# A 248-column product whose result nobody reads, placed ahead of groups of four transposes

## What is computed

```
x = x + squared_relu_mlp(rmsnorm(x, mlp_norm_g[i]), mlp_w_up[i], mlp_w_down[i])   # first model
m = jax.nn.silu(c) @ ada_w + ada_b        # second model: 6 x 1024 modulation columns per layer
```

## Time and profile before

| | |
|---|---|
| median of 3 runs | 1195.76 us (1193.81 to 1197.41) |
| profiled execution, its own time | 1202.31 us |
| its span, first to last instruction | 1200.7 us |
| TensorE busy (matmul rows) | 1185.0 us, 99% of the span |
| VectorE busy | 863.5 us, 72% |
| ScalarE busy | 636.0 us, 53% |
| granted TensorE clock, mean | 0.999 |

### The profile page before, as it was taken

The page is one execution under the profiler, slowest core; times in us unless marked ns, Lnnn a source line. Parts: engine busy times, 40 slices in busy tenths (PEclk is TensorE's granted clock), DMA queues, the critical chain, the costliest instruction groups (busy, mean ns, idle before and its releaser), DMA issues.

```text
span 1200.7 us, 23381 instructions
## 1 busy us (share of the span) xinstructions
PE 1185.0 (99%) x9643; PEld 1148.8 (96%) x9643; DVE 863.5 (72%) x1143; ACT 636.0 (53%) x853; POOL 95.4 (8%) x147
## 2 busy tenths in 40 slices
PE   8999999999999999999999999999999999999998
PEld 8999999999998999999999999999988779999998
DVE  5776887778776897777899888886476557755443
ACT  7557566634447567634468464333455665543432
POOL 0000010110124011110200001110000000000000
PEclk9999999999999999999999999999999999999999
DMA  9442587887772588787844648876745406565361
GB/s 335 159 175 72 178 290 269 297 291 253 263 263 72 176 270 291 277 289 275 294 171 141 203 149 281 286 254 204 235 142 193 157 1 187 166 210 178 124 193 66
DMA packets 150009, 249.98 MB, mean 208 GB/s; under 512 B 5505, under 2 KB 80618, under 8 KB 149930
## 3 DMA queue, kind: packets, MB, share of 16 engines
q1 hardware_dynamic: 135810, 198.21, 49.1%
q0 software_dynamic: 13952, 50.60, 11.7%
q10 hardware_dynamic: 168, 0.04, 0.0%
HBM read 247.79 MB, written 1.05 MB: 207 GB/s over the span
## 4 chain that ended last, share of the span: by engine, by line
PE 88%; DVE 8%; ACT 2%; issue 1%; ACTq 0%; POOL 0%; DVEq 0%
PE ps L2137 26%; PE ps L2139 26%; PE ps L2138 26%; DVE w_lo L1252 4%; PE ps L2405 2%; PE ps L2275 1%; PE ps L2693 1%; DVE scratch L1729 1%; PE ps L2387 1%; PE ps L2191 1%; ACT h_both L804 1%; PE ps L2667 1%; PE ps L2374 1%; PE ps L2707 1%; PE ps L2218 0%
## 5 line engine op out<-in xcount | busy, mean ns | idle before, releaser
L1252 DVE TENSOR_TENSOR w_lo<-raw,w_hi 128x2048 fp32r<-128x2048 f32 (+4 forms) x196 | 412.6, 2144 | 103.0 <-ACT w_hi L737 102.8
L737 ACT ACTIVATE w_hi<-raw 128x2048 fp32r<-128x2048 f32 (+4 forms) x196 | 342.0, 1790 | 169.0 <-PE ps L2139 168.9
L2137 PE MATMUL ps<-h_both,w_hi 128*128 128x256 f32 (+1 forms) x1296 | 363.8, 281 | 2.9 <-issue 1.1
L2139 PE MATMUL ps<-h_both,w_lo 128*128 128x256 f32 (+1 forms) x1296 | 361.3, 279 | 0.0
L2138 PE MATMUL ps<-h_both,w_hi 128*128 128x256 f32 (+1 forms) x1296 | 361.3, 279 | 0.0
L2137 PEld LDWEIGHTS ps<-h_both,w_hi 128*128 128x128 f32 (+1 forms) x1296 | 242.7, 187 | 4.3 <-issue 3.8
L2138 PEld LDWEIGHTS ps<-h_both,w_hi 128*128 128x128 f32 (+1 forms) x1296 | 244.2, 188 | 0.1
L2139 PEld LDWEIGHTS ps<-h_both,w_lo 128*128 128x128 f32 (+1 forms) x1296 | 244.1, 188 | 0.0
L2137 PE MATMUL ps<-a_both,w_hi 128*128 128x256 f32 x864 | 242.1, 280 | 0.0
L2139 PE MATMUL ps<-a_both,w_lo 128*128 128x256 f32 x864 | 241.4, 279 | 0.0
L2138 PE MATMUL ps<-a_both,w_hi 128*128 128x256 f32 x864 | 241.3, 279 | 0.0
(11 more groups left out here) (420 smaller groups left out, 1823.6 us busy)
## 6 DMA issues: line engine op xcount, KB each, us to landing
ada_raw<-in_l_ada_w POOLq DMA_DIRECT2D x96, 512.0 KB, 6.7
raw<-in_mlp_w_up SPq DMA_DIRECT2D x32, 1024.0 KB, 6.9
raw<-in_mlp_w_down SPq DMA_DIRECT2D x32, 1024.0 KB, 6.8
raw<-in_l_ffn_w_gate SPq DMA_DIRECT2D x22, 1024.0 KB, 5.4
raw<-in_l_ffn_w_up SPq DMA_DIRECT2D x22, 1024.0 KB, 8.0
raw<-in_l_ffn_w_down SPq DMA_DIRECT2D x16, 768.0 KB, 6.0
raw<-in_l_w_qkv SPq DMA_DIRECT2D x12, 1024.0 KB, 7.0
raw<-in_l_w_in SPq DMA_DIRECT2D x10, 1024.0 KB, 6.5
```

The lines of the kernel that those rows point to most:

```text
L737: nc.scalar.activation(w_hi[:, s.slot, cut], raw[:, s.slot, cut], ACT.Copy).then_inc(split_hi, 1)
L1252: nc.vector.tensor_tensor(w_lo[:, s.slot, cut], raw[:, s.slot, cut], w_hi[:, s.slot, cut].bitcast(F32), ALU.subtract).then_inc(split_lo, 1)
L2137: nc.tensor.matmul(to, sh, mh, start=first, stop=False, skip_group_check=True)
L2139: return nc.tensor.matmul(to, sl, mh, start=False, stop=last, skip_group_check=True)
```

## The change

`ada_reduce` takes an optional pair of operands. If it is given, one more matrix instruction is issued behind the semaphore wait and before the four transposes: a float32r product of 248 columns into bank 7, where the first transposes then overwrite it. Nothing reads it. It is given in the loops of `two_bank_slot` with `reduce` and in the down product: 6 groups in the two up products, 8 in the two down products, 4 in the gate/up product of the third layer, 18 of 24 in all. Its stationary operand is the first block of the slot's `w_hi`, its moving one a chunk of the rounded activations that the products around it use. The six other groups (one before slot 1 and one behind the down product in each MLP, group 9, group 23) stay as they are.

```diff
-            def ada_reduce(group):
+            def ada_reduce(group, unread=None):
 
                 pe.wait_ge(ada_step, group * 8 + 8)
+                if unread is not None:
+
+                    w, x = unread
+                    nc.tensor.matmul(ps[:, ADA_BANK, 0:T - 8], w, x[:, 0:T - 8], start=True, stop=True, skip_group_check=True)
                 for q in range(4):
                     ins = nc.tensor.transpose(ps[:, ADA_BANK, q * P:(q + 1) * P],
                                               scratch[:, 2 + q // 2, (q % 2) * P:(q % 2 + 1) * P], ident[:, :])
...
                     if b and reduce is not None:
-                        ada_reduce(reduce)
+                        ada_reduce(reduce, (ring(w_hi, s.slot, s.kc, s.cols)[:, 0, 0:P], hi[:, 0, :]))
...
                             if b == 1 and j % 2 == 0:
-                                ada_reduce(ADA_GROUP[f"down{l}"] + 2 * i + j // 2 - 1)
+                                ada_reduce(ADA_GROUP[f"down{l}"] + 2 * i + j // 2 - 1,
+                                           (ring(w_hi, s.slot, s.kc, s.cols)[:, 0, 0:P], a_hi[:, KD * j, :]))
```

## The result

The changed kernel takes 1205.79 us (median of 8 runs, 1201.98 to 1210.4) against 1197.7 us for the one before (8 runs); the ratio is 1.0069 with a 95% interval of 1.0049 to 1.0090. The forecast was 1190.3 with a range up to 1202, so the sign was wrong and the time outside the range. The rival "all stretches slow" had said 1204.2.

What follows compares the result with a forecast made beforehand. TensorE, running back to back, was taken to bound the kernel. Added products +2.04 us, slow stretches turned fast -7.6 and products behind a down product turned slow +0.2 gave -5.4: 1190.3 us from the 1195.76 median, range 1187.5 to 1202.

Steps and rivals of the forecast that it cites:

- all stretches slow: Rival: product plus transposes leave the slow rhythm behind every changed group; +8.4 us, 1204.2 us; chance 0.15.
- it costs 0.11 us: Each of 18 added products, between back-to-back TensorE work, costs 0.113 us like a 256-column product; +2.04 us in all.
- The two rhythms: Between groups, TensorE's products follow each other every 113.5 or 117.7 ns; 0.80 us per stretch of 192 products.
- an unchanged group entered fast leaves slow: Behind the first layer's down product, the unchanged group makes 54 products up to the norm sum slow; +0.2 us.
- the term of -7.6 us: Slow stretches become fast if all 18 groups keep the fast rhythm: 6.0 us in both MLPs, 1.6 in the SwiGLU.
- One instruction more ahead of them changes just that: At the 18 groups, the added product changes how the transposes are entered, on which the outcome hangs.
- the likeliest case: The fast rhythm survives each of the 18 groups; 1190.3 us, own range 1188.5 to 1192.5; chance 0.43.
- The premise itself: At groups of four transposes, the rhythm behind hangs on how they are entered, finer than the pace shows.
- I take the near row: The 248-column product is priced like its 256-column neighbours, 0.113 us; bounds 0.108 and 0.42 us each.
- 1.8 us of spread between runs: Allowance either way around the likeliest case, giving 1188.5 to 1192.5 us.
- a change of pace in the last SwiGLU: Sign: the last SwiGLU, counted as untouched, changing pace would make the forecast wrong by a missing term; no size given.
- The rule of the Trainium skill: Warm products lie N/2.4 + 2.5 ns apart; 18 added ones cost 1.9 us, nothing comes back, end at 1197.7 us.

Runs made afterwards that it cites:

- e1: Kernel before with the four transposes of the 18 groups left out and the semaphore wait kept; ratio to before 0.9909.
- e2: Changed kernel with a 256-column unread product and no transposes at the 18 groups; ratio to before 0.9967.
- e14: Kernel before plus four unread transposes, without a product, in the middle of slot 2 of the last SwiGLU; ratio to before 1.0051.
- e3: Changed kernel with 256 instead of 248 columns in the unread product; ratio to before 1.0005.
- e5: Changed kernel with the 248-column product only in the ten groups of the up and gate/up products; ratio to before 1.0042.
- e6: Changed kernel with 128 instead of 248 columns in the unread product; ratio to before 0.9962.
- e10: Changed kernel with 64 instead of 248 columns in the unread product; ratio to before 0.9974.
- e8: Changed kernel with the 248-column product behind the four transposes instead of ahead, into bank 6; ratio to before 0.9962.
- e15: Changed kernel with 192 instead of 248 columns in the unread product; ratio to before 0.9983.
- e12: The changed kernel with 248 columns run again, unaltered, for a second trace; ratio to before 1.0052.
- e11: Changed kernel with 128 columns, the product also given to the groups behind the down products and group 23 (21 groups); ratio to before 0.9956.
- e16: 128-column product in 21 groups, plus one such unread product and four unread transposes in slot 2 of the last SwiGLU; ratio to before 0.9994.
- e18: The kernel of e16 with a second unread 128-column product and four transposes, in slot 3 of the last SwiGLU; ratio to before 0.9905.
- e13: Kernel before plus an unread 128-column product and four unread transposes in the middle of slot 2 of the last SwiGLU; ratio to before 1.0005.

## Why the prediction was wrong

**Right:** TensorE's stream is the path, nothing hides or delays the added product, and it costs 0.11 us (2.0 us in all). The two rhythms are real, they are worth 0.8 us per stretch of 192 products, and the transposes tip them (e1, e2, e14). That an unchanged group entered fast leaves slow came true only in part: the group behind the first down product did so in e1, e2, e3, e5, e6 and e10, and with 128 columns the 54 products behind it turned slow as forecast, but in e8 and e15 it left fast. The term is 0.2 us.

**The step that failed** is the one that the term of -7.6 us hung on: "One instruction more ahead of them changes just that", and from there to the likeliest case that the fast rhythm survives each group. The first half is true of 248 columns, hardly of 256, and the second doesn't follow. With 248 columns each of nine fast entries in its two traces was tipped, and 21 of 27 groups entered in the slow rhythm left it in place. That adds slow stretches, 14 and 16 of 18 where before had 10, so the term came out as a loss of some 4 us and not a gain of 7.6: in the first trace 3.2 us for the four slow stretches more, and 0.6 around them. The premise itself, that all hangs on how the transposes are entered, is only half of it: e8 leaves the entry as it was and changes the outcome by what follows. I had two outcomes from two different entries, and no row at all that showed which way a changed entry would go; I gave 0.43 to the good one because it would repeat. It does repeat, with 128 columns. The rival on the other side had its price nearly right, +8.4 against the measured +8.1, but partly by luck: four stretches stayed fast in the one trace and two in the other, the first trace accounts for 5.8 us, the repetition e12 measured 0.5% (6.2 us), and the interval of the first measurement goes from 5.9 to 10.8 us.

**The width** was treated as a matter of price alone, "I take the near row". A step of eight columns changes the price by nothing that can be measured, and the rhythm entirely: 8 slow stretches with 256, 14 and 16 with 248, 10 with 240, none with 128.

**The noise.** I took 1.8 us of spread between runs. The last SwiGLU alone moves an execution by 6 us, and the profiled execution of before, 6.5 us over the median shown with it, was a sign of that which I used only as an offset. The prediction had named a change of pace in the last SwiGLU as a term that it hadn't got. The base moved as well: the median of before is 1197.7 over eight runs, 1.9 us above the three shown, so of the 15.5 us between forecast and result 13.5 are the wrong effect.

**The rule of the Trainium skill** that I weighed in the prediction, a distance by column count alone, would have given 1197.7. It misses the result by 8 us, 1.9 of them by the base, for the same reason for which it didn't fit. I had also taken it for more than it says: the Trainium skill's page "TensorE: Matmul & The Clock Gate", section "Back-to-back issue gap", calls the formula that of a single product, and says that in a stream of loads and products both set the distance. A second distance for the same instruction, as this case has it, isn't in it.

**Left open:** what the two rhythms are physically, and so why the fast one is lost. The traces show paces, entries and outcomes, not a mechanism. Nothing here tells why 240 and 248 columns differ from 256, why the same four transposes tip one fast stretch and not another, or how many phases each rhythm has.

## What to carry to other kernels

If TensorE runs back to back, compare the start distance of one and the same instruction across stretches of the trace, not its busy share. If there are two values, look for the odd instruction at which they change and try a few variants of what stands next to it (shorter, behind instead of ahead) on the chip: the direction can't be read off the trace of before. An effect of this kind also splits the run times into clusters, so judge a variant by its trace and by the clusters, and not by one median.

## What was new about the hardware

- One float32r product of 128x128 by 256 columns has two stable start distances at a granted clock of 1.00: 113.5 and 117.7 ns by the rows (113.3 and 117.8 within a stretch, to the nanosecond). 1343 of them in a row kept either (e1).
- Four float32 transposes mostly turn the fast one into the slow one (10 of 10 of the 18 groups before, 46 of 51 plain groups over all traces, but 12 of 37 behind a norm sum), and mostly the reverse. Entered slow, 37 of 38 turned fast where the first transpose began 120 ns behind the last product, none of 12 at 121 ns.
- A product of 64 to 192 columns ahead of them kept the fast one in 47 of 47 cases (e6, e10, e15), and one of 128 in the 69 of the 18 groups that were entered fast in e11 and e16 to e18; one of 248 columns lost it in 17 of 17 (four kernels' traces), and kept it in 17 of 17 behind them.
- After a wait in which two starts lay 0.58 us apart, and at the start of the last SwiGLU, TensorE resumed in either rhythm, in one program from one execution to the next (the 48 products behind that wait in the second MLP are fast in the trace of before and slow in that of e13, where the programs don't differ yet; the last SwiGLU is fast in the one trace of the changed kernel and slow in the other).
